# Weights of a one-core transformer kernel in units of 1 MB instead of 512 KB: one transfer and one split for two units, in three slots of twice the size

## What is computed

```python
def reference(x, ...):
    x = first_block(x, ...)
    return second_block(x, ...)

def first_block(x, ...):
    h = rms_norm(x, g_mix_pre)
    u, q, k, v = split(h @ w_in)
    y = concatenate([pool_mixer(u), moba_attention(q, k, v, rel_bias)]) @ w_out
    x = x + rms_norm(y, g_mix_post)
    h = rms_norm(x, g_ffn_pre)
    x = x + rms_norm(conv_ffn(h, w_up, conv_w, conv_b, w_down), g_ffn_post)
    return x + (p @ w_ple) * sigmoid(x @ w_ple_gate)

def second_block(x, ...):
    for layer in range(2):
        if layer % 2 == 0:
            b_g, c_g, h, q, k, v = split_cols(x @ ev_w_in, EVEN_SPLITS)
            y = concatenate([short_conv_mixer(b_g, c_g, h), swa_sink_attention(q, k, v, sinks)]) @ ev_w_out
        else:
            gq, gk, gv, g_low, gr, c_q, c_kv, k_r = split_cols(x @ od_w_in, ODD_SPLITS)
            y = concatenate([gla_mixer(gq, gk, gv, g_low, gr), mla_mixer(c_q, c_kv, k_r)]) @ od_w_out
        x = layer_norm(ALPHA * x + y)
        x = layer_norm(ALPHA * x + (silu(x @ w_gate) * (x @ w_up)) @ w_down)
    return x
```

## Time and profile before

| | us |
|---|---|
| median of 3 runs | 1013.54 |
| lowest and highest run | 1012.83, 1014.61 |
| span of the profiled execution | 1010.7 |
| PE busy | 944.9 |
| DVE busy | 669.1 |
| ACT busy | 421.5 |

### The profile page before, as it was taken

One profiled execution on the slowest core, in us unless ns is written; L12 is line 12 of the kernel. 1 busy time (PEld: TensorE's weight loads), 2 busy tenths in 40 slices (PEclk: granted clock), 3 DMA queues, 4 the chain that ended last, 5 costly groups with the idle time before them and its releaser, 6 DMA issues.

```text
span 1010.7 us, 19135 instructions
## 1 busy us (share of the span) xinstructions
PE 944.9 (93%) x7332; PEld 912.9 (90%) x7332; DVE 669.1 (66%) x1108; ACT 421.5 (42%) x628; POOL 34.2 (3%) x48
## 2 busy tenths in 40 slices
PE   6999799999998999988999999969979799999995
PEld 5987799999998999868999999969869699999994
DVE  5857787777777847778555555686986765555555
ACT  6245534444443644544333333247343343333332
POOL 1000000000000000000000000002401000000000
PEclk9999799999998999997999999979989799999997
DMA  7752155555553655322555555515313155555521
GB/s 284 265 171 92 63 170 197 182 184 176 178 183 105 208 173 164 123 84 90 183 185 186 175 181 184 187 41 173 121 42 124 44 167 184 176 181 185 187 83 42
DMA packets 43989, 154.73 MB, mean 153 GB/s; under 512 B 5072, under 2 KB 5802, under 8 KB 43946
## 3 DMA queue, kind: packets, MB, share of 16 engines
q1 hardware_dynamic: 42192, 151.12, 45.0%
q10 hardware_dynamic: 1449, 1.94, 0.6%
q0 software_dynamic: 304, 1.06, 0.4%
HBM read 153.04 MB, written 1.06 MB: 152 GB/s over the span
## 4 chain that ended last, share of the span: by engine, by line
PE 67%; issue 22%; DVE 7%; ACT 3%; DMA 1%; POOL 1%; SPq 0%; POOLq 0%; ACTq 0%; DVEq 0%
PE ps L349 18%; PE ps L350 17%; PE ps L351 17%; PE ps L366 1%; PE ps L533 1%; PE ps L373 1%; PE ps L367 1%; DVE w_lo L1052 1%; PE ps L649 1%; PE ps L408 1%; PE ps L410 1%; PE ps L409 1%; PE ps L450 1%; PE ps L421 1%; DMA raw<-in_stream 1%
## 5 line engine op out<-in xcount | busy, mean ns | idle before, releaser
L1052 DVE TENSOR_TENSOR w_lo<-raw,w_hi 128x1024 fp32r<-128x1024 f32 x284 | 341.2, 1223 | 191.1 <-ACT w_hi L768 190.4
L349 PE MATMUL ps<-op_hi,w_hi 128*128 128x256 f32 x1336 | 378.5, 283 | 0.0
L350 PE MATMUL ps<-op_lo,w_hi 128*128 128x256 f32 x1336 | 378.1, 283 | 0.0
L351 PE MATMUL ps<-op_hi,w_lo 128*128 128x256 f32 x1336 | 378.1, 283 | 0.0
L768 ACT ACTIVATE w_hi<-raw 128x1024 fp32r<-128x1024 f32 x284 | 288.7, 1051 | 67.5 <-PE ps L351 54.1
L349 PEld LDWEIGHTS ps<-op_hi,w_hi 128*128 128x128 f32 x1336 | 256.5, 192 | 1.0 <-DVE w_lo L1052 0.6
L350 PEld LDWEIGHTS ps<-op_lo,w_hi 128*128 128x128 f32 x1336 | 256.5, 192 | 0.0
L351 PEld LDWEIGHTS ps<-op_hi,w_lo 128*128 128x128 f32 x1336 | 256.5, 192 | 0.0
L349 PE MATMUL ps<-mix_hi,w_hi 128*128 128x256 f32 x748 | 216.4, 289 | 1.6 <-issue 1.4
L350 PE MATMUL ps<-mix_lo,w_hi 128*128 128x256 f32 x748 | 212.8, 284 | 0.0
L351 PE MATMUL ps<-mix_hi,w_lo 128*128 128x256 f32 x748 | 212.6, 284 | 0.0
(11 more groups left out here) (225 smaller groups left out, 817.1 us busy)
## 6 DMA issues: line engine op xcount, KB each, us to landing
raw<-in_stream SPq DMA_DIRECT2D x284, 512.0 KB, 3.4
x<-in_x SPq DMA_DIRECT2D x4, 256.0 KB, 6.2
y<-bias_rows POOLq DMA_DIRECT2D x1, 1024.0 KB, 8.5
result<-x SPq DMA_DIRECT2D x4, 256.0 KB, 2.5
proj<-in_gmask ACTq DMA_DIRECT2D x1, 512.0 KB, 5.4
masks<-in_masks ACTq DMA_DIRECT2D x1, 384.0 KB, 4.6
wpool<-in_wpool ACTq DMA_DIRECT2D x1, 256.0 KB, 3.8
pt<-in_p ACTq DMA_DIRECT2D x1, 256.0 KB, 4.7
```

The source lines that it names most:

```text
L349: pe.matmul(o, wh, xh, start=start, stop=False, **kw)
L350: pe.matmul(o, wh, xl, start=False, stop=False, **kw)
L351: return pe.matmul(o, wl, xh, start=False, stop=stop, **kw)
L1052: dve.tensor_tensor(w_lo[:, s, :], raw[:, s, :], fp(w_hi[:, s, :]), ALU.subtract).then_inc(S["split_done"], 1)
```

## The change

`UNIT` stays 1024 columns, but `raw`, `w_hi` and `w_lo` become three slots of 2048 columns, that is of two units (the space is the same). One transfer brings two units, 1 MB, one ACT instruction of 128x2048 rounds them and one DVE instruction of 128x2048 subtracts. A slot's semaphores count pairs. Of the steps only those of odd n split: step n splits the pair of units n+3 and n+4 (n+1 and n+2 in the third feed-forward). Before the first step two pairs are split, where four units were. PE waits for the pair that its unit is in, and ACT for the last unit of the pair that had the slot of `w_hi` before (three pairs back).

```diff
--- before.py
+++ after.py
 UNIT = 1024
-SLOTS = 6
+SLOTS = 3
...
-        raw = sb("raw", [P, SLOTS, UNIT])
-        w_hi = sb("w_hi", [P, SLOTS, UNIT], F32R)
-        w_lo = sb("w_lo", [P, SLOTS, UNIT], F32R)
+        raw = sb("raw", [P, SLOTS, 2 * UNIT])
+        hi_pairs = sb("w_hi", [P, SLOTS, 2 * UNIT], F32R)
+        lo_pairs = sb("w_lo", [P, SLOTS, 2 * UNIT], F32R)
+        w_hi = hi_pairs[:, :, :].rearrange("p s (u n) -> p (s u) n", u=2)
+        w_lo = lo_pairs[:, :, :].rearrange("p s (u n) -> p (s u) n", u=2)
...
             sp.dma_start(pair(x, 0), pair(d["x"], 0)).then_inc(x_loaded[0], 16)
-            sp.dma_start(raw[:, 0, :], d["stream"][0]).then_inc(raw_loaded[0], 16)
+            def both(v):
+                return d["stream"][2 * v:2 * v + 2].rearrange("a p n -> p a n")
+
+            def slot(s):
+                return raw[:, s, :].rearrange("p (a n) -> p a n", a=2)
+
+            sp.dma_start(slot(0), both(0)).then_inc(raw_loaded[0], 16)
             for i in range(1, 4):
...
             for s in range(1, SLOTS):
-                sp.dma_start(raw[:, s, :], d["stream"][s]).then_inc(raw_loaded[s], 16)
-            rounds = UNITS // SLOTS
+                sp.dma_start(slot(s), both(s)).then_inc(raw_loaded[s], 16)
+            rounds = UNITS // 2 // SLOTS
             with sp.Fori(1, rounds) as r:
-                at = [sp.snap(r * SLOTS + s) for s in range(SLOTS)]
+                at = [sp.snap(r * (2 * SLOTS) + 2 * s) for s in range(SLOTS)]
                 for s in range(SLOTS):
...
                     sp.wait_ge(S["split_done"], r * SLOTS + (s - SLOTS + 1))
-                    sp.dma_start(raw[:, s, :], d["stream"][bass.ds(at[s], 1)].rearrange("a p n -> p (a n)")
+                    sp.dma_start(slot(s), d["stream"][bass.ds(at[s], 2)].rearrange("a p n -> p a n")
                                  ).then_inc(raw_loaded[s], 16)
-            for v in range(rounds * SLOTS, UNITS):
+            for v in range(rounds * SLOTS, UNITS // 2):
                 sp.wait_ge(S["split_done"], v - SLOTS + 1)
-                sp.dma_start(raw[:, v % SLOTS, :], d["stream"][v]).then_inc(raw_loaded[v % SLOTS], 16)
+                sp.dma_start(slot(v % SLOTS), both(v)).then_inc(raw_loaded[v % SLOTS], 16)
...
+            def split_ready(more):
+
+                n = unit.n + more
+                pairs = n // 2 + 1
+                pe.wait_ge(S["split_done"], pairs if unit.turn is None else unit.turn * (unit.per // 2) + pairs)
+                return n % (2 * SLOTS)
+
             def take():
-                pe.wait_ge(S["split_done"], unit.at(1))
-                return unit.n % SLOTS
+                return split_ready(0)
...
-                slots = (unit.n % SLOTS, (unit.n + 1) % SLOTS)
+                slots = (unit.n % (2 * SLOTS), (unit.n + 1) % (2 * SLOTS))
                 for part in (((0,), (1,)) if operand == 0 else ((0, 1),)):
-                    pe.wait_ge(S["split_done"], unit.at(part[-1] + 1))
+                    split_ready(part[-1])
                     for k in range(NCH):
...
                 if split.turn is not None or split.n >= SLOTS:
-                    act.wait_ge(S["units_done"], split.at(1 - SLOTS))
-                act.activation(w_hi[:, s, :], raw[:, s, :], ACT.Copy).then_inc(S["split_hi_done"], 1)
+                    done = 2 * (split.n - SLOTS + 1)
+                    act.wait_ge(S["units_done"], done if split.turn is None else split.turn * (2 * split.per) + done)
+                act.activation(hi_pairs[:, s, :], raw[:, s, :], ACT.Copy).then_inc(S["split_hi_done"], 1)
                 split.n += 1
...
-                if ahead:
+                if ahead and unit.n % 2 == 1:
                     split_hi()
...
                     unit.enter(i, 6)
-                    split.enter(i, 6)
+                    split.enter(i, 3)
                     step()
...
                     split_hi()
-            for _ in range(3):
+            for _ in range(1):
                 split_hi()
...
                 dve.wait_ge(S["split_hi_done"], split.at(1))
-                dve.tensor_tensor(w_lo[:, s, :], raw[:, s, :], fp(w_hi[:, s, :]), ALU.subtract
+                dve.tensor_tensor(lo_pairs[:, s, :], raw[:, s, :], fp(hi_pairs[:, s, :]), ALU.subtract
                                   ).then_inc(S["split_done"], 1)
...
             def step(ahead=True):
-                if ahead:
+                if ahead and unit.n % 2 == 1:
                     split_lo()
...
                     unit.enter(i, 6)
-                    split.enter(i, 6)
+                    split.enter(i, 3)
                     own.count.enter(i, per)
...
                     split_lo()
-            for _ in range(3):
+            for _ in range(1):
                 split_lo()
```

4 lines of the change are left out of this document (2 added, 2 removed).

## The result

| | before | after |
|---|---|---|
| median, us (4 runs each) | 1013.18 | 1059.38 |
| lowest and highest | 1012.53, 1014.61 | 1058.21, 1060.19 |
| span of the profiled execution | 1010.7 | 1058.2 |

The ratio is 1.0454, with a 95% interval of 1.0439 to 1.0469. The change costs 46.2 us where 35.3 were forecast; 1059.4 lies in the range (1039 to 1062), above the likeliest case's own (1039 to 1058).

A forecast was written before the change was run, and what follows sets the result against it. PE was taken to bound the kernel, busy 944.9 of 1010.7 us. Third feed-forward 28.7, start 2.1, odd layer 2.5 and norms 2.0 make 35.3 us; on 1013.5 that gives 1049 us, range 1039 to 1062.

The forecast's parts named there:

- likeliest case: The prediction's own sum for the whole kernel: 1049 us, own range 1039 to 1058, chance 0.74.
- wait A: Third feed-forward: PE waits for a pair whose ACT split stands behind the gate's activation; 1.88 us, 11 times, 20.7 us.
- wait B: Third feed-forward: PE waits for the next gate unit's pair, subtracted by DVE after the chunk's product; 0.80 us, 10 times.
- falls of the clock there: Third feed-forward: drops of PE's granted clock to 0.50 behind its waits; none in the sum, 1.45 us each if they came.
- start: Kernel's head: the first pair lands and is split later, first matmul at 12.5 instead of 9.35; net +2.1 us.
- two norms, and unit 214: Behind the second feed-forward and third attention: last pairs delay DVE's norms, and unit 214's pair is late; +2.0 us.
- odd layer's projection, up to unit 214: Units 192 to 207: pairs come late behind ACT's activation and DVE's scans, delaying the last evacuation; +2.5 us.
- elsewhere: Attention 1 and 2, even layer, first two feed-forwards: three units of PE work cover the later split; 0 us.
- What bounds and what moves: Whole kernel: PE bounds it; pairs begin a step later and are ready only whole, with one unit's lead in feed-forward three.
- the rival of the clock: Third feed-forward: the clock falls after each of 11 waits of 1.88 us, +16 us, 1065 us; chance 0.18.
- The price of a pair: One 128x2048 split, extrapolated from 512 and 1024 columns: ACT 1.89 us, DVE 2.30; 4.28 from ACT's start to PE.
- The other rivals: Feed-forward waits do not form, 1020 us, chance 0.05; wide splits are cheap enough, 1011 us, chance 0.03.

The follow-up runs named there:

- lead kept: The changed kernel, but the third feed-forward splits the same distance ahead as the first two, leaving out no steps at its start: 1025.5 us, ratio 1.0125.

## Why the prediction was right, and where it was off

| term | forecast | measured |
|---|---|---|
| wait A, 11 times | 1.88 each, 20.7 | 1.97 (2.03 at the first and the last), 21.9, less 0.3 that came back just ahead of the first: 21.6 |
| wait B, 10 times | 0.80 each, 8.0 | 0.97 (the first 0.89), 9.6 |
| falls of the clock there | 0 | two, 3.0 |
| start | 2.1 | 3.8 |
| two norms, and unit 214 | 2.0 | 0.9 + 1.3 = 2.2 |
| odd layer's projection, up to unit 214 | 2.5 | 4.5 |
| elsewhere | 0 | 2.7 |
| sum | 35.3 | 47.4 |

**What bounds and what moves.** Both held. In the stages that were called covered PE waits for no split, and the two places in the third feed-forward were the right ones, in number too: without them (lead kept) the kernel loses 12, not 46 us. The size was forecast too low: every term came out larger, so no error hid another, and 1059.4 is above the likeliest case's own range. It lies in the stated one because that range had been drawn up to 1062 for the rival of the clock, two of whose falls are 3.0 us of the excess.

The prediction put 2.8 us between the span and the device time for what lies around it. That compared the span of one execution with the median of others; within one execution it is 2.0 us for the changed kernel (1060.19 and 1058.2). The sum starts from the median, so it doesn't change.

**The price of a pair** was right: ACT 1.91 us (1.89 forecast), DVE 2.29 (2.30). Extending the line through 512 and 1024 columns was good to 1%.

**Waits A and B** were each 0.1 short, since PE restarts slowly. The first matmul behind a wait A is late by 1.88 us, exactly as forecast; it is recorded with 0.39 us, and the third starts 0.34 after it, not 0.24. B was another 0.1 short because DVE starts its split 1.42 us after PE's boundary, 877.34 to 878.76, not 1.32.

**Start.** The weights were ready for ACT at 9.18, not at 8.25. I had added the time of 512 KB at the rate of the earlier trace rows to the landing of unit 0; the first `x` was late by 0.9 us as well (ACT's first rounding of `x` at 6.54, 5.68 before). What it measured is 2.2 us in place of 1.3, and the first matmul is at 13.47, not 12.5. Behind it the estimate failed as well: of the 3.15 us of the first matmul 1.05 were to come back, and only 0.3 of 4.1 did. The wait for the second unit (0.70 us at 13.71 before) is gone as worked out. But the slow spacing of 0.21 us at the head of the kernel lasts until 18.49, for 7 matmuls more than the 16 taken. It is the spacing of a clock at 0.50 (the same 0.21 us at 909), though the views write 1.00 there, as in the earlier trace rows. How long it lasts is not a property of the change: from the first matmul on it is 4.6 us in the trace of the kernel before, 5.0 here, and between 2.9 and 6.3 in the 13 traces.

**Odd layer.** The chain that was worked out is the one that ran; PE waits 1.72 us for the evacuation, and goes on at 718.11:

```profile
718.11 0.79 PE L422 MATMUL ps<-w_hi,op_hi 128*128 128x512 f32 x1 [1.72 <-DVE proj L1496]
```

That is 10.85 us after 707.26, with 7.4 lost before the layer, so 3.4 against 2.5: the evacuation started at 717.64, where 709.4 + 7.4 = 716.8 was forecast. Of the 3.4 us 0.7 came in before the chain, between 670 and 680 us, where the clock is at 0.50 for 13.7 us behind the norm (from 666.9) and was for 10.2 before (from 661.3); the chain itself is 2.7. The rest, to 4.5, is spread over the gates and the attention behind it. I had booked them at nothing, and falls of the clock stand at other places there in the two traces (718 and 766 us, against 736 and 753), so this last 1 us was not taken apart.

**Elsewhere: 2.7, forecast 0.** This is the step that failed. I had asked whether the pair is ready for PE in the stages that I named, and neither in the first projection nor for the other work that waits for DVE. Four pieces make 2.1 of the 2.7 us (places by the time in the kernel before):

- 0.6 at 26 us, in the first projection: PE does wait for a pair, whose subtraction starts behind the projection's own work on DVE.
- 0.55 at 130 us, for the statistics beside the first feed-forward. PE waits for a small instruction of GpSimd, and that takes 2.67 us beside the wide subtraction and 1.60 beside two narrow ones; at 464 us of the changed kernel, where no split runs beside it, it takes 0.74. The changed kernel (first four lines) and the one with narrow subtractions (last two):

```profile
132.04 2.28 DVE L1067 TENSOR_TENSOR w_lo<-raw,w_hi 128x2048 fp32r<-128x2048 f32 x1
132.21 2.67 POOL L271 TENSOR_TENSOR tok_rinv<-tok_var,minus_half 128x2 f32<-128x2 f32 x1 [14.06 <-DVE tok_var L1116]
134.94 0.18 POOL L276 COPY tok_ffn<-tok_rinv 128x2 f32<-128x2 f32 x1
135.18 0.71 PE L464 MATMUL ps<-ident,tok_rinv 128*128 128x128 f32 x4 [0.28 <-POOL tok_ffn L276]
...
130.98 2.35 DVE L1068 TENSOR_TENSOR w_lo<-raw,w_hi 128x1024 fp32r<-128x1024 f32 x2
131.15 1.60 POOL L272 TENSOR_TENSOR tok_rinv<-tok_var,minus_half 128x2 f32<-128x2 f32 x1 [14.00 <-DVE tok_var L1117]
```

- 0.4 at 462 us, behind the even layer's norm. No split is near it, and its cause stays open.
- 0.6 at 431 us, in the even layer's attention. The softmax's statistics on DVE stand behind the pair.

The first three are in all seven traces whose subtractions are wide outside the loops, and in none of the five where they are narrow. The fourth is not a matter of width: it is there with narrow subtractions too (two of 1024 columns take 2.35 us at one step, one of 2048 takes 2.29), in every kernel that splits two units at one step, and it is gone only with 1 MB transfers alone, where each step splits one. The run with narrow subtractions loses 0.4 us from 17.64 to 462, but that is a net figure: it loses the 0.6 at 431 and gains 0.8 behind the norm at 320 us, where its clock is at 0.50 for 3.4 us in place of 6.8.

**Rivals.** The first (the clock falls at each wait A, 1065) was right in what one fall costs (1.45 forecast, 1.5 measured) and wrong in how often: two of 11. The Trainium skill ("TensorE: Matmul & The Clock Gate", HAM oscillation), whose pattern it was, has a loop throttled at every turn, with waits for data of about 3 to 5 us in its example; this trace, with waits of 1.7 to 1.8 us, shows it at two turns of 11, and at none with wait A at 0.90. The gap at 454.06 was a weak witness against the rival: the window of the earlier trace rows ends at 456.00, and right behind it the clock of the kernel before is at 0.50 too:

```profile
456.60:466.00 9.40, 6.38 (x28) 6.03 (x29) 7.72 (x21) 4.07 (x9) 0.74 (x1) 0.50 0.00 0
```

The other rivals did not occur. That merging transfers saves time, as the Trainium skill advises ("DMA: Bandwidth & Descriptors", rules for kernel authors), no run here shows: 1014.7 us against 1013.6 with 142 fewer transfers.

## What to carry to other kernels

Merging two instructions in a chain of engines (transfer, rounding, subtraction, matmul) saves the engines time and lengthens the way of the first half: here 0.12 us less of DVE's time a pair (341.2 less 324.8 us over 142 pairs), and 1.9 us more before PE can start (4.28 against 2.36). Before merging, count for every stage how many units lie between a split and its use, and put that time against the merged chain and what stands ahead of it on each engine; keep the last link before the consumer narrow and let the consumer start on its first half, since that gave back 27 of the 46 us alone. And ask of every stage that uses the merged engine itself who stands behind the longer instruction, or waits beside it as GpSimd did here, even where the product of the merge is in time.

## What was not expected

- A restart of PE behind a wait of 0.7 to 1.8 us costs 0.1 us beyond the wait, at the full granted clock.
- The clock fell at two of 11 nearly equal waits (1.72 us idle, the first and the last 1.81), in three traces at the same two, and at others when the stage began earlier. Between variants the time at 0.50 in the whole trace differed by up to 21 us (58 to 79), part of it after the last matmul of a weight; that moves the span by a few us, so differences of 0.2 to 0.3% between variants are not read here.
- Two transfers of 512 KB, with another 768 KB issued between them, brought the first pair 2.35 us later than one of 1 MB, and at the end of the trace only 0.4 of it was left.
- One and the same GpSimd operation on 128x2 elements took 0.74 us with no split beside it on DVE, 1.60 beside two subtractions of 1024 columns and 2.67 beside one of 2048.
- The first matmuls of every trace start 0.21 us apart and later ones 0.12, with the change of pace 2.9 to 6.3 us after the first matmul. A forecast of the start to better than 1 us is luck.
